# The gated recurrence of a three-layer kernel: one-level chunks of 64 tokens for two-level chunks of 128

## The reference

```python
def gla_chunk_scan(q, k, v, g):
    """S_t = diag(exp(g_t)) S_{t-1} + k_t v_t^T ; o_t = S_t^T q_t, chunkwise."""
    ...
        G = jnp.cumsum(gi, axis=-2)
        G_last = G[..., -1:, :]
        q_dec = qi * jnp.exp(G)
        k_inv = ki * jnp.exp(-G)
        k_end = ki * jnp.exp(G_last - G)
        attn = jnp.where(mask, jnp.einsum('bhik,bhjk->bhij', q_dec, k_inv), 0.0)
        o = (jnp.einsum('bhij,bhjv->bhiv', attn, vi)
             + jnp.einsum('bhik,bhkv->bhiv', q_dec, state))
        new_state = (jnp.exp(G_last[..., 0, :])[..., None] * state
                     + jnp.einsum('bhjk,bhjv->bhkv', k_end, vi))
```

## Time and profile before

| | us |
|---|---|
| median of 3 runs | 2498.62 (2497.88 to 2499.41) |
| the profiled execution: its time | 2498.62 |
| its span, first to last instruction | 2496.7 |
| PE, DVE, POOL, ACT busy | 2335.3, 1492.5, 1354.1, 654.2 |
| mean granted clock of TensorE | 0.967 |

### The profile page before, as it was taken

The page is one execution under the profiler, slowest core; times in us unless marked ns, Lnnn a source line. Parts: engine busy times, 40 slices in busy tenths (PEclk is TensorE's granted clock), DMA queues, the critical chain, the costliest instruction groups (busy, mean ns, idle before and its releaser), DMA issues.

```text
span 2496.7 us, 26088 instructions
## 1 busy us (share of the span) xinstructions
PE 2335.3 (94%) x10372; PEld 1884.4 (75%) x10372; DVE 1492.5 (60%) x1824; ACT 654.2 (26%) x1196; POOL 1354.1 (54%) x818
## 2 busy tenths in 40 slices
PE   7999979999988899999899999889997999999997
PEld 5888857888876577777678888768665777878786
DVE  6785748245466666165765376678745445736455
ACT  3442332100013354154211011231434132202111
POOL 5455355666665344445466666476331835656563
PEclk9999999999999899999999999999997999999999
DMA  4222222333332111112233333233110422323332
GB/s 150 77 68 85 59 82 75 93 101 93 99 95 68 36 36 50 54 36 64 72 104 99 95 114 96 75 101 91 53 51 17 127 68 74 96 87 99 92 92 78
DMA packets 59448, 200.02 MB, mean 80 GB/s; under 512 B 6592, under 2 KB 9920, under 8 KB 59328
## 3 DMA queue, kind: packets, MB, share of 16 engines
q1 hardware_dynamic: 56160, 194.69, 26.0%
q10 hardware_dynamic: 3168, 3.67, 0.5%
HBM read 196.24 MB, written 2.10 MB: 79 GB/s over the span
## 4 chain that ended last, share of the span: by engine, by line
PE 83%; DVE 10%; ACT 3%; POOL 2%; issue 1%; DMA 1%; DVEq 0%; SPq 0%; POOLq 0%; ACTq 0%
PE bank L402 25%; PE bank L403 25%; PE bank L404 25%; DVE uL L1661 2%; POOL wL L2397 1%; PE bank L881 1%; DVE F L1669 1%; DVE tmp L1661 1%; DVE mq L1661 1%; PE bank L433 1%; POOL wH L2395 1%; PE bank L751 1%; PE bank L756 1%; DVE h L1661 1%; PE bank L757 1%
## 5 line engine op out<-in xcount | busy, mean ns | idle before, releaser
L2395 POOL TENSOR_SCALAR wH<-raw 128x1024 fp32r<-128x1024 f32 (+3 forms) x375 | 404.5, 1079 | 984.4 <-PE bank L404 966.4
L2397 POOL TENSOR_TENSOR wL<-raw,wH 128x1024 fp32r<-128x1024 f32 (+3 forms) x375 | 906.6, 2418 | 31.3
L402 PE MATMUL bank<-aH,wH 128*128 128x512 f32 x1520 | 608.5, 400 | 61.5 <-ACT aH L1097 31.7
L403 PE MATMUL bank<-aL,wH 128*128 128x512 f32 x1520 | 598.6, 394 | 0.0
L404 PE MATMUL bank<-aH,wL 128*128 128x512 f32 x1520 | 598.2, 394 | 0.0
L402 PE MATMUL bank<-uH,wH 128*128 128x512 f32 x960 | 384.4, 400 | 29.7 <-DVE uL L1661 22.3
L402 PEld LDWEIGHTS bank<-aH,wH 128*128 128x128 f32 x1520 | 289.7, 191 | 134.4 <-issue 22.6
L403 PE MATMUL bank<-uL,wH 128*128 128x512 f32 x960 | 380.3, 396 | 0.0
L404 PE MATMUL bank<-uH,wL 128*128 128x512 f32 x960 | 380.0, 396 | 0.0
L403 PEld LDWEIGHTS bank<-aL,wH 128*128 128x128 f32 x1520 | 289.6, 191 | 61.9 <-issue 2.8
L404 PEld LDWEIGHTS bank<-aH,wL 128*128 128x128 f32 x1520 | 288.9, 190 | 61.4
(11 more groups left out here) (304 smaller groups left out, 3125.5 us busy)
## 6 DMA issues: line engine op xcount, KB each, us to landing
raw<-in_ws SPq DMA_DIRECT2D x341, 512.0 KB, 3.6
raw<-in_ws SPq DMA_DIRECT2D x16, 384.0 KB, 3.1
raw<-in_ws SPq DMA_DIRECT2D x9, 256.0 KB, 2.7
h<-in_xT SPq DMA_DIRECT2D x4, 512.0 KB, 7.0
E<-in_memT ACTq DMA_DIRECT2D x16, 128.0 KB, 2.9
out<-c_F SPq DMA_DIRECT2D x8, 256.0 KB, 2.2
raw<-in_ws SPq DMA_DIRECT2D x8, 192.0 KB, 2.4
tmp<-in_pT ACTq DMA_DIRECT2D x4, 256.0 KB, 2.9
```

The source lines that it names most:

```text
L402: P.e.matmul(o, lH, rH, start=start, stop=False, skip_group_check=skip)
L403: P.e.matmul(o, lH, rL, start=False, stop=False, skip_group_check=skip)
L2395: G.e.tensor_scalar(wH[n % NW][:, c], raw[n % NR][:, c], 1.0, 0.0, MUL, ADD).then_inc(*G.did("wH", n, i))
L2397: G.e.tensor_tensor(wL[n % NW][:, c], raw[n % NR][:, c], wH[n % NW][:, c].bitcast(F32), SUB).then_inc(*G.did("w", n, i))
```

## The change

Chunks become 64 tokens long with one level: eight chunks, seven states passed on per direction, and the scan's sums are used as they are. The mask of the scores keeps two blocks of 64 in each 128x128 tile. In the extract below the parts stand in this order: constants, PE's recurrence and outputs, ACT, DVE's decay sums and states. All eight decays, all four transposed key tiles and all 512 columns of g_ke and g_kT are made. U becomes seven matmuls over 64 rows, which alternate between the two halves of the partitions and between two banks, both of them given back when DVE has made the last state. The queries times states become seven matmuls of 64 columns per direction. g_mid and g_end are gone.

```diff
-    part("mask_f")[:] = j <= i
-    part("mask_b")[:] = j >= i
+    part("mask_f")[:] = (j // 64 == i // 64) & (j <= i)
+    part("mask_b")[:] = (j // 64 == i // 64) & (j >= i)
...
-            g_St = [sb(f"g_St{d}", [128, 3, 128], F32, st) for d in range(2)]
+            g_St = [sb(f"g_St{d}", [128, 7, 128], F32, st) for d in range(2)]
...
-                    for n in g_order[d][0:3]:
+                    for n in range(4):
                         i = P.e.transpose(b.ap[:, cols128(n)], g_ke[d][:, cols128(n)], ident)
...
-                    b = take("U", head, d)
+                    order = list(range(8)) if d == 0 else list(range(7, -1, -1))
+                    ub = [take("U", head, d, half) for half in range(2)]
                     P.wait_ge(A, "kT", head, d)
                     P.wait_ge(A, "Vt", head // 4, 3)
-                    for j in range(3):
-                        n = g_order[d][j]
-                        i = P.e.matmul(b.ap[:, cols128(j)], g_kT[d][:, cols128(n)], g_Vt[:, n, vc], start=True, stop=True)
-                    i.then_inc(*P.did("U", head, d))
-                    give(b, V, "St", head, d, 2)
+                    for j in range(7):
+                        half = order[j] % 2
+                        n, r, x = order[j] // 2, half_rows(half), 128 * (j // 2)
+                        i = P.e.matmul(ub[half].ap[:, x:x + 128], g_kT[d][r, cols128(n)], g_Vt[r, n, vc], start=True, stop=True)
+                        if j >= 5:
+                            i.then_inc(*P.did("U", head, d, half))
+                    for b in ub:
+                        give(b, V, "St", head, d, 6)
...
-                    for j in range(1, 4):
-                        c = cols128(g_order[d][j])
+                    for j in range(1, 8):
+                        c = slice(64 * order[j], 64 * order[j] + 64)
...
+                gl = g_G[d][:, slice(63, 512, 64) if d == 0 else slice(0, 512, 64)]
-                do(g_dec[head % 2][d][:, g_on[d]], g_end[d][:, g_on[d]], ACT.Exp).then_inc(*A.did("dec", head, d))
+                do(g_dec[head % 2][d][:, :], gl, ACT.Exp).then_inc(*A.did("dec", head, d))
...
-                    do(g_kT[d][:, g_onc[d]], bk("keT", head, d)[:, g_onc[d]], ACT.Copy).then_inc(*A.did("kT", head, d))
+                    do(g_kT[d][:, :], bk("keT", head, d)[:, :], ACT.Copy).then_inc(*A.did("kT", head, d))
...
-                V.e.tensor_copy(g_mid[d][:, :], G3[:, :, mid]).then_inc(*V.did("mid", head, d))
...
-                tt(g_end[d][:, g_on[d]], G3[:, g_on[d], end], after, ADD).then_inc(*V.did("end", head, d))
...
-                tt(G3[:, :, first], G3[:, :, first], g_mid[d][:, :].unsqueeze(2).to_broadcast([128, 4, 64]), SUB).then_inc(
-                    *V.did("G", head, d))
...
-                    for j in range(1, 3):
-                        n = g_order[d][j]
+                    for j in range(1, 7):
+                        c, x = order[j], 128 * (j // 2)
+                        V.wait_ge(P, "U", head, d, c % 2)
                         V.wait_ge(V, "St", head, d, j - 1)
```

More of the change, by code:

```diff
@@ L280, in build @@
             g_qd = [[sb(f"g_qd{i}{d}", [128, T], F32, st) for d in range(2)] for i in range(2)]
-            g_dec = [[sb(f"g_dec{i}{d}", [128, 4], F32, st) for d in range(2)] for i in range(2)]
-            g_mid, g_end = ([sb(f"g_{n}{d}", [128, 4], F32, st) for d in range(2)] for n in ("mid", "end"))
+            g_dec = [[sb(f"g_dec{i}{d}", [128, 8], F32, st) for d in range(2)] for i in range(2)]
             g_nol = sb("g_nol", [128, 8], F32, st)
-            g_St = [sb(f"g_St{d}", [128, 3, 128], F32, st) for d in range(2)]
+            g_St = [sb(f"g_St{d}", [128, 7, 128], F32, st) for d in range(2)]
         g_scan = g_hc[:, 0:2 * T].rearrange("p (d t) -> p d t", d=2)
         g_mask = g_hc[:, 2 * T:].rearrange("p (d j) -> p d j", d=2)
-        g_order = [[0, 1, 2, 3], [3, 2, 1, 0]]
-        g_on = [slice(0, 3), slice(1, 4)]
-        g_onc = [slice(0, 384), slice(128, 512)]
         C, Sn = sb("C", [128, T]), sb("Sn", [128, T])
@@ L557, in outputs @@
                 for d in range(2):
-                    for j in range(1, 4):
-                        c = cols128(g_order[d][j])
+                    order = list(range(8)) if d == 0 else list(range(7, -1, -1))
+                    for j in range(1, 8):
+                        c = slice(64 * order[j], 64 * order[j] + 64)
                         P.wait_ge(V, "St", head, d, j - 1)
-                        i = P.e.matmul(b.ap[:, c], g_St[d][:, j - 1, :], g_qd[head % 2][d][:, c], start=False, stop=d == 1 and j == 3,
+                        i = P.e.matmul(b.ap[:, c], g_St[d][:, j - 1, :], g_qd[head % 2][d][:, c], start=False, stop=d == 1 and j == 7,
                                        skip_group_check=True)
@@ L1148, in decays @@
             def decays(head, d):
+                gl = g_G[d][:, slice(63, 512, 64) if d == 0 else slice(0, 512, 64)]
                 A.wait_ge(V, "G", head, d)
                 if head > 1:
-                    A.wait_ge(V, "St", head - 2, 1, 2)
-                do(g_dec[head % 2][d][:, g_on[d]], g_end[d][:, g_on[d]], ACT.Exp).then_inc(*A.did("dec", head, d))
+                    A.wait_ge(V, "St", head - 2, 1, 6)
+                do(g_dec[head % 2][d][:, :], gl, ACT.Exp).then_inc(*A.did("dec", head, d))
                 if head:
@@ L1759, in log_decay @@
                     V.wait_ge(A, "eq", head - 1, d)
[L1760 to L1763, removed]
                 if d == 0:
-                    V.e.tensor_tensor_scan(G, g_scan[:, 0, :], g_f[0][:, :], 0.0, MUL, ADD).then_inc(*V.did("sum G", head, d))
-                else:
-                    V.e.tensor_tensor_scan(G[:, ::-1], g_scan[:, 1, ::-1], g_f[1][:, ::-1], 0.0, MUL, ADD).then_inc(
-                        *V.did("sum G", head, d))
-                V.wait_ge(V, "sum G", head, d)
-                V.e.tensor_copy(g_mid[d][:, :], G3[:, :, mid]).then_inc(*V.did("mid", head, d))
-                V.wait_ge(V, "mid", head, d)
-                after = g_mid[d][:, slice(1, 4) if d == 0 else slice(0, 3)]
-                tt(g_end[d][:, g_on[d]], G3[:, g_on[d], end], after, ADD).then_inc(*V.did("end", head, d))
-                V.wait_ge(V, "end", head, d)
-                tt(G3[:, :, first], G3[:, :, first], g_mid[d][:, :].unsqueeze(2).to_broadcast([128, 4, 64]), SUB).then_inc(
-                    *V.did("G", head, d))
+                    V.e.tensor_tensor_scan(g_G[0][:, :], g_scan[:, 0, :], g_f[0][:, :], 0.0, MUL, ADD).then_inc(
+                        *V.did("G", head, d))
+                else:
+                    V.e.tensor_tensor_scan(g_G[1][:, ::-1], g_scan[:, 1, ::-1], g_f[1][:, ::-1], 0.0, MUL, ADD).then_inc(
+                        *V.did("G", head, d))
             def keys(head, d):
@@ L1784, in keys @@
                     V.wait_ge(P, "keT", head - 1, d)
-                tt(g_ke[d][:, g_onc[d]].rearrange("p (n j) -> p n j", j=128), g_ki[d][:, g_onc[d]].rearrange("p (n j) -> p n j", j=128),
-                   g_dec[head % 2][d][:, g_on[d]].unsqueeze(2).to_broadcast([128, 3, 128]), MUL).then_inc(*V.did("ke", head, d))
+                tt(g_ke[d][:, :].rearrange("p (c j) -> p c j", j=64), g_ki[d][:, :].rearrange("p (c j) -> p c j", j=64),
+                   g_dec[head % 2][d][:, :].unsqueeze(2).to_broadcast([128, 8, 64]), MUL).then_inc(*V.did("ke", head, d))
             def queries(head, d):
@@ L1798, in recur @@
                                         bk("S", head, d)[:, :].rearrange("p (n j) -> p n j", j=128)).then_inc(*V.did("Ab", head, d))
[L1799 to L1803, removed]
+                    order = list(range(8)) if d == 0 else list(range(7, -1, -1))
+                    ub = [bk("U", head, d, half) for half in range(2)]
+                    V.wait_ge(P, "U", head, d, order[0] % 2)
+                    V.e.tensor_copy(g_St[d][:, 0, :], ub[order[0] % 2][:, 0:128]).then_inc(*V.did("St", head, d, 0))
                     V.wait_ge(A, "dec", head, d)
-                    for j in range(1, 3):
-                        n = g_order[d][j]
+                    for j in range(1, 7):
+                        c, x = order[j], 128 * (j // 2)
+                        V.wait_ge(P, "U", head, d, c % 2)
                         V.wait_ge(V, "St", head, d, j - 1)
-                        stt(g_St[d][:, j, :], g_St[d][:, j - 1, :], g_dec[head % 2][d][:, n:n + 1], ub[:, cols128(j)], MUL, ADD).then_inc(
+                        stt(g_St[d][:, j, :], g_St[d][:, j - 1, :], g_dec[head % 2][d][:, c:c + 1], ub[c % 2][:, x:x + 128], MUL, ADD).then_inc(
                             *V.did("St", head, d, j))
```

## The result

The changed kernel is slower by 1%: 2524.24 us median of 4 runs (2522.54 to 2525.02), against 2498.25 us for the kernel before; ratio 1.0104, 95% interval 1.0087 to 1.0121. The forecast was 2522.8, the range 2513 to 2534. The profiled execution took 2522.2 us on a span of 2520.4, against 2498.62 and 2496.7.

The account below looks back on a forecast made before the run. PE was taken to bound the head loop, with DVE covered. Seven heads at +2.86 us (20.0) plus 4.2 in the last head gave +24.2 on 2498.6, so 2522.8 us, range 2513 to 2534.

Parts of the forecast that it names:

- Head 7: Last head: with fewer banks, PE's second U waits about 1.4 us for DVE's direction 0 states; +4.2 us in all.
- Heads 0 to 6: First mixer's head loop: PE pays 1.07 + 1.79 = 2.86 us more a head, 20.0 us over seven heads.
- Part 1: Queries times states on PE: 28 instead of 12 records a head at 0.112 us each, +1.79 us a head.
- Part 2: State updates U on PE: 14 records pair into eight slots, +0.23 us each; three row changes at 0.13, +0.39 a head.
- Rival 1: U's 64-row matmuls do not pair in fp32: 14 slots, +10.7 us, 2533.5 us; chance 15%.
- Part 3: Fourth transpose on PE and longer first key copy on ACT, 0.11 us each: sum +0.22 us a head.
- Stays hidden: ACT's second key copy, though longer, has 0.9 us of PE's scores over it and costs nothing.
- Part 4: DVE's eight more state steps a head, +2.92 us before g_As, stay covered with 0.35 us left; PE pays nothing.
- repays the 2.92: DVE operations removed after g_As offset the 2.92 us of added state steps, so the next head's inputs are not late.
- Rival 3: DVE paces the head loop, so its net of -1.36 us a head counts: -9.5 us, 2489.1 us; chance 2%.
- 2: Rival: 64-column query-state matmuls on PE cost by their columns, 1.57 us a head less: -12.6 us, 2510.2 us; chance 7%.
- 4: Rival: something swallows the whole effect and the time stays within 5 us; chance 3%.

Follow-up runs that it names:

- the halves in sequence: Changed kernel with U's seven matmuls ordered four on one half of the partitions, then three on the other: 2529.25 us, 1.0116 of the kernel before.
- the run on all rows: Changed kernel with all 128 rows in each of U's seven matmuls, so no change of rows; timing only: 2532.11 us, 1.0130 of the kernel before.
- DVE's work put back: Changed kernel with DVE's three removed operations per direction after the scan put back in the same sizes: 2525.60 us, 1.0105 of the kernel before.
- the short states: Changed kernel with states 3 to 6 of each direction made on 8 of 128 columns; timing only: 2523.15 us, 1.0095 of the kernel before.

## Why the prediction was right

**The whole.** 24.2 us forecast, 23.7 in the profiled pair, 26.0 between the medians. The agreement of the profiled pair is closer than it deserves. From the first transpose of head 0 (77.01 before, 79.50 after) to the last query-state record of head 7 (319.32 and 345.24) it is +23.4 us. Outside, the execution after lost 2.5 us before head 0, where nothing was changed, and won 2.2 behind head 7; in the ten profiles of this study the first transpose of head 0 starts anywhere from 76.4 to 79.8 us. That is the noise of single executions, not the change. Seven periods of +3.01 and head 7's +4.4 make 25.5, near the 26.0 of the medians and 1.3 above the forecast; that the profiled pair shows 2 less is luck (under Head 7).

**Heads 0 to 6, per head.** Starts of PE's matmul groups in head 2, before and after: waiting and copy 1.99 to 2.09 (+0.10, forecast 0.11); first U 0.77 to 1.09 (+0.32; 0.36 with its change); transposes 0.33 to 0.49 (+0.16; 0.11); scores 0.89 to 0.99 (+0.10; a change at 0.13); second U and projection 6.16 to 6.70 (+0.54; 0.36); outputs and the rest 19.46 to 21.25 (+1.79; 1.79). Sum +3.01, forecast 2.86. The list puts 0.54 on the second U and only 0.10 on the scores ahead of it because the second U's first matmul starts together with its load (149.34), where before it started 0.11 behind (140.21, load at 140.10). By starts of loads:

```profile
138.88 0.36 PEld L529 LDWEIGHTS bank<-cs,g_ke 128*128 128x128 f32 x3
139.21 0.97 PEld L536 LDWEIGHTS bank<-g_qd,g_ki 128*128 128x128 f32 x8
140.10 0.75 PEld L545 LDWEIGHTS bank<-g_Vt,g_kT 128*128 128x128 f32 x6
140.78 0.19 PEld L402 LDWEIGHTS bank<-aH,wH 128*128 128x128 f32 x1
```

First U 0.66 to 1.08, transposes 0.33 to 0.39, scores 0.89 to 1.10, second U 0.68 to 1.08: +0.42, +0.06, +0.21, +0.40, together 1.09 for the 0.96 forecast. The mis-sized terms are the change of rows behind each U, 0.20 for 0.13, and what stands between the scores and the second U, 0.21 for 0.13. Against that the transposes cost 0.06 for 0.11, and the slots of a U a few hundredths less than forecast.

**Part 1** (queries times states, 0.112 us a record) is right to the hundredth and shown from both sides. One reading in it is off: the eight records of the earlier trace rows belong to four matmuls of one column, two records each, not to eight matmuls. The price of a record stays as read.

**Part 2.** Eight slots are right; the reason I gave for eight was not the whole, since the halves in sequence took 11 and not 13. Rival 1 (no pairing in fp32) fell with the profile and with the run on all rows.

**Part 3.** The first copy cost what was forecast. "Stays hidden" for the second is doubtful: 0.13 us ahead of the second U remain in the run without a change of rows.

**Part 4.** That DVE is covered is right, and the 0.35 us of cover forecast are 0.43, or 0.38 without the handover of 0.05 that the forecast took off. The claim that what goes "repays the 2.92" was wrong in size. DVE's busy time in the period rose by 0.93 us, from 26.19 to 27.12, where the earlier trace rows gave -1.36. The long means of g_G and g_mid were mostly not their own work. In head 2 before, the first g_G took 0.42 us with POOL idle, the second 2.50 beside POOL's split of a weight tile:

```profile
145.67 0.42 DVE L1661 TENSOR_TENSOR g_G<-g_G,g_mid 128x256 f32<-128x256 f32 x1
...
148.15 2.39 POOL L2397 TENSOR_TENSOR wL<-raw,wH 128x1024 fp32r<-128x1024 f32 x1
148.32 2.50 DVE L1661 TENSOR_TENSOR g_G<-g_G,g_mid 128x256 f32<-128x256 f32 x1
```

After, the operations that now stand beside wL (157.66 to 160.81) are the long ones: the second scan takes 1.99 us for 1.22 before, the first g_ki 2.79 for 0.68. That POOL is what holds them is read from this coincidence; no run took POOL's work away. Rival 3's price was wrong with it.

**Head 7.** Forecast +4.2, measured from its first transpose to its last query-state record 14.71 for 10.29, +4.4; the new wait 1.25 us where 1.4 was forecast. No stretch at the lower clock followed it: the granted clock is 1.00 from 330.5 to 346 us. The one that before's profile had ahead of head 7 is absent after, as the windows of the same work show (the granted clock is the first number behind POOL's count), first before, then after:

```profile
296.00:309.00 13.00, 11.21 (x42) 8.72 (x41) 4.99 (x6) 3.18 (x4) 2.37 (x1) 0.87 0.15 40
```

```profile
318.00:330.50 12.50, 11.03 (x47) 8.51 (x46) 4.56 (x5) 3.87 (x5) 3.41 (x2) 1.00 0.13 44
```

In the run with DVE's work put back, on the same code there, it is back at 0.88 (317.0 to 331.2 us). So it comes and goes with the execution; it makes head 6's period grow by 1.1 us instead of 3.0 in the profiled pair, which hides about 2 us of the change's price there.

**Rivals.** 2 fell with two runs, 3 with the short states and the work put back, 4 with the result.

## What to carry to other kernels

Count records, not columns: here a plain fp32 matmul with a new stationary operand costs 0.11 us for each of its two records, whether it has 1, 64 or 128 moving columns. So halving a chunk about doubles the price of the products whose stationary side is the chunk's state. Read an engine's busy time beside a competing engine as work plus something that may be waiting; here that part did not leave with the operation. And write down how much cover a change uses up, even where the period doesn't show it: the next gain on the other engine will meet it.

## What was not expected of the hardware

Matmuls of 64 rows on the two halves of the array overlap even when the program has all of one half ahead of the other: 14 fp32 records took 11 slots of 0.11 us, not 13. A change from 64 to 128 rows cost 0.20 us behind each U, 0.15 in the later attention. And the length of a step on DVE hardly falls with its columns: 0.35 us at 128 and 0.22 at 8.
